# Index heads scored in pairs between the products of a gate projection, and the index's last 72 columns computed feature-major

## What is computed

```python
q, k, v, z, qi, ki, wi = jnp.split(xn @ w_in, cuts, axis=-1)   # 4 x 1024, 8 x 64, 64, 8 columns
qi = concat([rope(qi[..., :32]), qi[..., 32:]])                # 8 index heads of 64
ki = concat([rope(ki[..., :32]), ki[..., 32:]])                # one index key of 64
wi = wi * (8 ** -0.5 * 64 ** -0.5)
rel = relu(einsum("qhd,sd->qhs", qi_b, ki_b))
score = einsum("qh,qhs->qs", w_b, rel)                         # per block of 128 queries
top_val, top_idx = top_k(where(chunk_visible, score, -inf), 128)
...                                                            # softmax attention over the picked keys
return (o * silu(z)) @ w_out
```

## Time and profile before

| | |
|---|---|
| median of 3 runs | 3107.18 us |
| profiled execution, first to last instruction | 3119.8 us |
| PE busy | 3027.5 us (97%) |
| DVE busy | 1790.2 us (57%) |
| POOL busy | 1547.0 us (50%) |
| ACT busy | 928.5 us (30%) |
| mean granted TensorE clock | 0.984 of full |

### The profile page before, as it was taken

One profiled execution on the slowest core, in us unless ns is written; L12 is line 12 of the kernel. 1 busy time (PEld: TensorE's weight loads), 2 busy tenths in 40 slices (PEclk: granted clock), 3 DMA queues, 4 the chain that ended last, 5 costly groups with the idle time before them and its releaser, 6 DMA issues.

```text
span 3119.8 us, 40047 instructions
## 1 busy us (share of the span) xinstructions
PE 3027.5 (97%) x15372; PEld 1965.7 (63%) x15516; DVE 1790.2 (57%) x3290; ACT 928.5 (30%) x1472; POOL 1547.0 (50%) x788
## 2 busy tenths in 40 slices
PE   8999999899999999998999999999999999999998
PEld 6888686688667887886778444455545444444444
DVE  6433398635653433014621999689995456655564
ACT  2001214623661012114222322343333332223222
POOL 5664268955015666466456443345644333443342
PEclk9998799999999999999999999999999999999999
DMA  3222122122332223222122434355555765556551
GB/s 146 108 81 96 44 108 71 26 97 71 132 139 108 108 85 125 95 81 102 55 108 101 183 139 157 149 229 216 202 202 228 243 215 203 191 198 215 208 193 57
DMA packets 139991, 429.99 MB, mean 138 GB/s; under 512 B 8800, under 2 KB 79584, under 8 KB 116704
## 3 DMA queue, kind: packets, MB, share of 16 engines
q1 hardware_dynamic: 125376, 353.40, 31.8%
q10 hardware_dynamic: 7200, 68.68, 5.3%
q0 software_dynamic: 7296, 6.31, 0.9%
HBM read 358.10 MB, written 73.40 MB: 138 GB/s over the span
## 4 chain that ended last, share of the span: by engine, by line
PE 86%; POOL 5%; DVE 4%; issue 3%; DMA 1%; ACT 1%; SPq 0%; DVEq 0%; ACTq 0%; POOLq 0%
PE bank L1140 13%; PE bank L1141 13%; PE bank L1142 13%; PE bank L691 4%; PE bank L692 3%; PE bank L694 3%; POOL rpb_tiles L2459 3%; PE bank L952 3%; PE bank L947 3%; PE bank L948 3%; PE bank L721 3%; PE bank L722 2%; PE bank L749 2%; PE bank L726 2%; PE bank L743 2%
## 5 line engine op out<-in xcount | busy, mean ns | idle before, releaser
L2504 POOL TENSOR_TENSOR work<-ring,work 128x4096 bf16<-128x4096 f32 x64 | 582.8, 9106 | 791.7 <-ACT work L1589 791.7
L1140 PE MATMUL bank<-work 128*128 128x512 bf16 x2005 | 761.1, 380 | 5.7 <-DVE work L2345 2.7
L1141 PE MATMUL bank<-work 128*128 128x512 bf16 x2005 | 761.4, 380 | 3.3 <-ACT work L1600 1.0
L1142 PE MATMUL bank<-work 128*128 128x512 bf16 x1990 | 755.6, 380 | 2.3
L2528 POOL CAST w_parts<-ring 128x1024 fp32r<-128x1024 f32 (+3 forms) x212 | 231.6, 1092 | 652.9 <-DMA ring<-in_wstream 150.6
L2530 POOL TENSOR_TENSOR w_parts<-ring,w_parts 128x1024 fp32r<-128x1024 f32 (+3 forms) x212 | 511.5, 2413 | 17.0
L2345 DVE TENSOR_TENSOR work<-hF,work 128x512 bf16<-128x512 f32 x128 | 307.8, 2405 | 252.5 <-ACT work L1674 249.4
L1142 PEld LDWEIGHTS bank<-work 128*128 128x128 bf16 x2048 | 200.6, 98 | 242.4 <-issue 1.4
L1140 PEld LDWEIGHTS bank<-work 128*128 128x128 bf16 x2048 | 200.7, 98 | 238.7 <-issue 4.7
L1141 PEld LDWEIGHTS bank<-work 128*128 128x128 bf16 x2048 | 200.6, 98 | 234.6 <-issue 1.4
L2313 DVE SCALAR_TENSOR_TENSOR work<-const,work 128x256 f16<-128x256 f32 x512 | 299.1, 655 | 30.0 <-PE bank L1164 29.8
(11 more groups left out here) (424 smaller groups left out, 4942.2 us busy)
## 6 DMA issues: line engine op xcount, KB each, us to landing
ring<-in_wstream SPq DMA_DIRECT2D x128, 2048.0 KB, 7.7
hidden<-hF ACTq DMA_DIRECT2D x32, 1024.0 KB, 3.9
gates<-work ACTq DMA_DIRECT2D x16, 2048.0 KB, 8.8
hF<-hidden SPq DMA_DIRECT2D x32, 1024.0 KB, 7.1
work<-gates SPq DMA_DIRECT2D x32, 1024.0 KB, 10.2
rpb_tiles<-in_rpb POOLq DMA_DIRECT2D x192, 16.0 KB, 2.3
work<-rpb_tiles POOLq DMA_DIRECT2D x24, 128.0 KB, 4.4
ring<-in_wstream SPq DMA_DIRECT2D x5, 512.0 KB, 4.0
```

The lines of the kernel that those rows point to most:

```text
L1140: pe.matmul(out, a(0), b(0), start=(start and k == 0), stop=False)
L1141: pe.matmul(out, a(0), b(1), start=False, stop=False)
L1142: mm = pe.matmul(out, a(1), b(0), start=False, stop=(stop and k == n - 1))
L2504: nc.gpsimd.tensor_tensor(SPLIT[:, p, 1, :], ring[:, p, :], SPLIT[:, p, 0, :], ALU.subtract).then_inc(lo, 1)
```

## The change

1. The last 72 index columns are computed feature-major: 72 weight columns stationary, 512 tokens streaming, into 72 rows of bank 4. There are 24 products in two chunks where there were 96. ACT copies the result to `idx_wide`, PE turns it back by four transposes behind gate chunk 0 (`turn_index_key`), and DVE copies it to `B_IDX`.
2. The index heads are turned two at a time into 128 rows, and the key is doubled (`idx_twice`), so that its transposes fill both halves. That makes 20 transposes in five groups where there were 36 in nine. Four groups stand between gate chunks 3 and 4, the fifth behind chunk 4.
3. The 24 scores become 12 pairs, one head on rows 0 to 63 and one on rows 64 to 127. A pair stands behind every fifth product of gate chunks 5 to 7, the last behind the 60th of their 72. ACT's list has the ReLUs between its Silus. DVE's adds and its selection are as before.

```diff
-        idx_q = area(8192, IDX_HEADS, S)
+        idx_q = area(8192, IDX_HEADS // 2, S)
+        idx_twice = area(10240, NT, 2 * IDX_DIM)
+        idx_wide = area(10752, S)
         idx_k = area(24192, S)
+        IDX_LAST = IDX_COLS - 512
+        IDX_PAIRS = (NT - 1) * IDX_HEADS // 2
+        PAIR_EVERY = 5
...
             def project_index():
                 c = CHUNK["b_idx"]
-                for m, (width, per) in enumerate(((512, 2), (72, 4))):
-                    for k in range(0, KT, per):
-                        token_chunk(c, (FIRST["b_idx"] + m) % 2, range(k, k + per), KT - 1, width, b_rounded, rest,
-                                    signal("b_idx_ready"), "b" if m == 0 else None)
-                        c += 1
-                        if m == 0:
-                            turn_fill("b", k // per)
+                for k in range(0, KT, 2):
+                    token_chunk(c, 0, range(k, k + 2), KT - 1, 512, b_rounded, rest, signal("b_idx_ready"), "b")
+                    c += 1
+                    turn_fill("b", k // 2)
+                out = bank[0:IDX_LAST, 4, :]
+                for ks in (range(4), range(4, KT)):
+                    w = chunk_parts(c, 4, IDX_LAST)
+                    pe.wait_ge(signal("parts_made"), c + 1)
+                    for k in ks:
+                        pe.matmul(out, w[0][:, k % 4, :], b_rounded[:, k, :], start=(k == 0), stop=False)
+                        pe.matmul(out, w[1][:, k % 4, :], b_rounded[:, k, :], start=False, stop=False)
+                    for k in ks:
+                        mm = pe.matmul(out, w[0][:, k % 4, :], rest[:, k, :], start=False, stop=(k == KT - 1))
+                    mm.then_inc(signal("parts_used"), 1)
+                    c += 1
+            def turn_index_key():
+
+                pe.wait_ge(signal("b_idx_by_act"), 3)
+                for t in range(NT):
+                    mm = pe.transpose(bank[:, 5, t * IDX_LAST:(t + 1) * IDX_LAST],
+                                      idx_wide[0:IDX_LAST, t * P:(t + 1) * P], ident[0:IDX_LAST, 0:IDX_LAST])
+                mm.then_inc(signal("b_idx_ready"), 1)
+            def turn_index_pair(i, b):
+
+                for t in range(NT):
+                    x = idx_twice[:, t, :] if i == 0 else B_IDX[:, t, (i - 1) * P:i * P]
+                    mm = pe.transpose(bank[:, b, t * P:(t + 1) * P], x, ident)
+                mm.then_inc(signal("idx_turned"), 1)
+            def score_index_pair(n):
+
+                qt, pair = 1 + n // (IDX_HEADS // 2), n % (IDX_HEADS // 2)
+                size = (qt + 1) * P
+                if n < 2:
+                    pe.wait_ge(signal("idx_turn_taken"), (2, 5)[n])
+                else:
+                    pe.wait_ge(signal("idx_relued"), 2 * n - 2)
+                for e in range(2):
+                    rows_ = slice(64 * e, 64 * e + 64)
+                    pe.matmul(bank[:, 2 * (n % 2) + e, 0:size], idx_q[rows_, pair, qt * P:(qt + 1) * P],
+                              idx_k[rows_, 0:size], start=True, stop=True).then_inc(signal("idx_scored"), 1)
+            def gate_and_index():
+
+                c0, by_act = CHUNK["b_in"], signal("b_in_by_act")
+
+                def gate(j):
+
+                    out, w, done = bank[:, j, :], chunk_parts(c0 + j, KT, P), 24 * (j - 5)
+
+                    def pair_behind(n):
+                        if j >= 5 and (done + n) % PAIR_EVERY == 0 and (done + n) // PAIR_EVERY <= IDX_PAIRS:
+                            score_index_pair((done + n) // PAIR_EVERY - 1)
+
+                    pe.wait_ge(signal("parts_made"), c0 + j + 1)
+                    for k in range(KT):
+                        pe.matmul(out, w[0][:, k, :], b_rounded[:, k, :], start=(k == 0), stop=False)
+                        pair_behind(2 * k + 1)
+                        pe.matmul(out, w[1][:, k, :], b_rounded[:, k, :], start=False, stop=False)
+                        pair_behind(2 * k + 2)
+                    for k in range(KT):
+                        mm = pe.matmul(out, w[0][:, k, :], rest[:, k, :], start=False, stop=(k == KT - 1))
+                        if k == KT - 1:
+                            mm.then_inc(signal("parts_used"), 1)
+                        pair_behind(2 * KT + k + 1)
+
+                for j in range(4):
+                    pe.wait_ge(signal("b_idx_by_act" if j < 2 else "b_idx_by_dve"), j % 2 + 1)
+                    gate(j)
+                    if j == 0:
+                        turn_index_key()
+                pe.wait_ge(signal("idx_rotated"), 1)
+                for i in range(4):
+                    pe.wait_ge(by_act, i + 1)
+                    turn_index_pair(i, i)
+                gate(4)
+                pe.wait_ge(signal("idx_turn_taken"), 3)
+                turn_index_pair(4, 2)
+                for j in range(5, 8):
+                    gate(j)
+                pe.wait_ge(signal("idx_relued"), 2 * IDX_PAIRS)
...
-            def index_scores():
...
-            pe.wait_ge(signal("b_idx_by_act"), 4)
-            pe.wait_ge(signal("b_idx_by_dve"), 4)
-            project_features("b_in", CHUNK["b_in"], FIRST["b_in"], b_rounded, rest)
-            index_scores()
+            gate_and_index()
             for i in range(1, 4):
                 project_b(i)
...
+            def move_index_key():
+
+                act.wait_ge(signal("parts_used"), CHUNK["b_idx"] + 6)
+                act.activation(idx_wide[0:IDX_LAST, :], bank[0:IDX_LAST, 4, :], ACT.Copy)\
+                    .then_inc(signal("b_idx_by_act"), 1)
+            def gate_and_index():
+
+                def gate(j):
+                    take_gate("b_in", "b_in", B_Z, [(j, j)])
+
+                def move(i, b):
+                    act.wait_ge(signal("idx_turned"), i + 1)
+                    act.activation(idx_q[:, i - 1, :] if i else idx_k, bank[:, b, :], ACT.Copy)\
+                        .then_inc(signal("idx_turn_taken"), 1)
+
+                def relus(pairs):
+                    for n in range(2 * pairs[0], 2 * pairs[-1] + 2):
+                        size = (2 + n // IDX_HEADS) * P
+                        act.wait_ge(signal("idx_scored"), n + 1)
+                        if n >= 2:
+                            act.wait_ge(signal("idx_added"), n - 1)
+                        act.activation(idx_rel[:, n % 2, 0:size], bank[:, n % 4, 0:size], ACT.Relu)\
+                            .then_inc(signal("idx_relued"), 1)
+
+                for j in range(4):
+                    gate(j)
+                for i in range(4):
+                    move(i, i)
+                gate(4)
+                move(4, 2)
+                for j in range(3):
+                    end = [min(24 * (x + 1) // PAIR_EVERY, IDX_PAIRS) for x in (j - 1, j)]
+                    relus(range(*end))
+                    gate(5 + j)
...
-            take_tokens("b_idx", lambda m, t: B_IDX[:, t, m * 512:m * 512 + [512, 72][m]], [512, 72])
-            take_gate("b_in", "b_in", B_Z, [(j, j) for j in range(8)])
-            index_scores()
+            take_tokens("b_idx", lambda m, t: B_IDX[:, t, 0:512], [512])
+            move_index_key()
+            gate_and_index()
...
-            take_tokens("b_idx", lambda m, t: B_IDX[:, t, m * 512:m * 512 + [512, 72][m]], [512, 72], [4, 6])
-            dve.wait_ge(signal("b_idx_by_act"), 4)
-            dve.wait_ge(signal("b_idx_by_dve"), 4)
+            take_tokens("b_idx", lambda m, t: B_IDX[:, t, 0:512], [512], [4])
+            dve.wait_ge(signal("b_idx_ready"), 4)
+            order(v.tensor_copy(B_IDX[:, :, 512:IDX_COLS],
+                                bank[:, 5, 0:NT * IDX_LAST].rearrange("p (t n) -> p t n", t=NT)))
+            dve.wait_ge(signal("b_idx_by_act"), 2)
+            dve.wait_ge(signal("b_idx_by_dve"), 2)
             for t in range(NT):
                 rope(B_IDX[:, t, 0:576].rearrange("p (h d) -> p h d", h=9)[:, :, 0:32], 16,
                      plain(trig[:, 2, t, 0:16], trig[:, 3, t, 0:16]), area(B_FREE, 576))
                 order(v.tensor_scalar(B_IDX[:, t, 576:584], B_IDX[:, t, 576:584],
                                       IDX_HEADS ** -0.5 * IDX_DIM ** -0.5, None, ALU.mult))
+            order(v.tensor_copy(idx_twice.rearrange("p t (a d) -> p t a d", a=2),
+                                B_IDX[:, :, 512:576].rearrange("p t (a d) -> p t a d", a=1)
+                                .broadcast_to([P, NT, 2, IDX_DIM])))
             dve.sem_inc(signal("idx_rotated"), 1)
             index_scores()
             selection()
```

More of the change, by code:

```diff
@@ L773, in project_b @@
                         token_chunk(c0 + 8 * (i - 1) + 4 * p + q, p, range(2 * q, 2 * q + 2), KT - 1, 512, b_rounded, rest, ready)
-            def index_scores():
[L777 to L796, removed]
-                pe.wait_ge(relued, n)
             def attention(a, modulated=()):
@@ L1410, in head_roots @@
                 act.activation(sums, sums, ACT.Sqrt, scale=1.0 / dim, bias=eps).then_inc(signal("heads_root"), 1)
-            def index_scores():
```

(17 more changed lines are left out.)

## The result

| | before | after |
|---|---|---|
| timed together, median (lowest to highest) | 3106.93 us (3102.97 to 3113.42), 5 runs | 3087.22 us (3083.80 to 3089.55), 5 runs |
| second time | 3109.14 us (3101.18 to 3124.43), 29 runs | 3088.54 us (3085.96 to 3093.74), 6 runs |
| profiled execution, span | 3119.8 us | 3087.7 us |
| its mean granted clock | 0.984 | 0.991 |

The ratio is 0.9927, interval 0.9902 to 0.9951, and the second time 0.9935, 0.9917 to 0.9952. The change saves 20 us. The forecast was 3072 us with a range of 3063 to 3084: direction right, time 15 us too low, outside the range.

The account below looks back on a forecast made before the run. PE was taken to bound the kernel, with 86% of the chain. Removing 103.8 us and adding 68.7 us gave 35.1 us less, off the 3107.2 us median: 3072 us, range 3063 to 3084.

Parts of the forecast that it names:

- Together 103.8 us: PE time removed: 72-column products 16.9, gate chunks with their wait 47.4, transposes 6.5, scores 30.0, slow start of `project_b` 3.0.
- 3.0 us of slow start: At the start of `project_b`: 16 products take 3.7 us warm but 6.7 us before the change, so 3.0 are lost.
- 24 products of 72 columns and the wait on POOL: Ahead of gate chunk 0: 5.5 us for the feature-major products, then 1.3 us waiting for POOL's parts.
- Five chunks and the transposes: Gate chunks 0 to 4 warm at 5.53 us each, 24 transposes at 3.3 us in all, and 0.3 us of waiting.
- The wait on `idx_rotated`: Before the head transposes: DVE ends near 301.1, PE arrives at 303.9; 0.3 us taken, bounds 0 and 3.
- 12 pairs: In gate chunks 5 to 7: 11.5 us from attention b's rows plus 2.4 us for neighbouring products, taken as 14.0 us.
- rival C: ACT and DVE set the pace of chunks 5 to 7, through adds held by POOL: gain 30, 3077 us, chance 0.09.
- rival B: Thin products or half-array scores bring 1.2 GHz again: one fall 3081 us, chance 0.10; chunks 5 to 7 whole 3103, 0.02.
- POOL late next: At `b_out`: attention b starts 1.4 us less early than POOL's chain, so PE's 3.65 us wait shrinks to about 2.3.
- Rival D: Each of 24 changes between full products and half-array scores stops PE far longer; at 2 us each 3118 us, chance 0.03.
- A: Within a pair the two heads run one after the other: pairs cost 22.6 us, gain 26.5, 3081 us, chance 0.12.
- B's single fall: The clock falls to 1.2 GHz once for some 17 us, costing 8.5: gain 26.6, 3081 us, chance 0.10.

Follow-up runs that it names:

- the profiles with 4 and 8 more products: Kernel before with 4 or 8 extra full products, later overwritten, ahead of the last 72 columns: medians 3109.89 and 3110.58 us, ratios 0.9997 and 1.0002.
- the second profile of after: The changed kernel run once more, unchanged, with a profile: median 3088.54 us in 6 runs, ratio 0.9935.
- its shifted kin: Kernel before with 4, 8 or 12 extra full products ahead of the last 72 columns: medians 3109.89, 3110.58 and 3110.93 us.
- the columns alone: Against before, only the 72 columns made feature-major, transposes and single-head scores kept in one block behind the gate: 3093.23 us, ratio 0.9946.
- the second profile: The kernel before run once more, unchanged, with a profile: median 3105.26 us in 12 runs, ratio 0.9997, profiled span 3123.8 us.
- the three spacings: The changed kernel with a pair behind every fifth product (3088.54 us again), every third (3086.99 us), or two pairs behind every tenth (3084.98 us).

## Why the prediction was wrong

**The step that failed** is "Together 103.8 us", with "I take the difference off it" behind it. The sum counted 30.0 us of scores and 3.0 us of slow start from one execution and subtracted them whole from a median that mostly does without them. The working even had the 12.6 us by which the profile exceeded the median, and called them a difference to be taken off both sides. They were most of the very cost that the sum then removed a second time. Like for like it was more, since a span is about 1.8 us short of a time: 3121.6 against 3107.2, 14.4 us. The term that was mis-sized is 29.32 us for the 24 scores, which take 15.76 at full clock, with the 3.0 us behind them, which are then nothing.

With the scores at full clock, as the profiles with 4 and 8 more products have them, what goes is 103.8 - 13.6 - 3.0 = 87.2 us. What comes is the forecast's 68.7. That makes 18.5 us, and 3107.2 - 18.5 = 3088.7, against 3087.2 and 3088.5 measured. With what the new stretch really takes, 6.74 + 30.26 + 29.33 = 66.3 us, it is 3086.3. Compared with the long runs of before alone, the change is worth nearly what was forecast: 3121.4 - 3088.5 = 32.9 us of 35.1. So is the stage: it takes 113.4 - 0.9 = 112.5 us in the kernel with 4 products more and 112.8 - 1.8 = 111.0 in that with 8, against 90.0 after, 21 to 22.5 us less. The rival that something outside takes the time back falls with it: `project_b` lost 2.9 us where the forecast had 3.0, and attention b grew by 0.5, at a clock of 0.90 instead of 0.95. In the second profile of after attention b took 104.8 us, at a clock of 0.87, yet that span is no longer (3086.8 us).

The 72-column products are the other piece at half clock, and there the profile could be trusted: the clock fell there in every profile of before and its shifted kin. So the 16.9 us and the slow start of gate chunk 0 behind them (7.9 us for it instead of 5.53, 2.4 us) went against 6.74, which makes 12.6 us, and the columns alone brought 12.7.

Point by point:

- *24 products of 72 columns and the wait on POOL*: 277.37 to 284.11, 6.74 us; forecast 6.8, with PE waiting 1.01 us where 1.3 stood.
- *Five chunks and the transposes*: 284.11 to 314.37, 30.26 us; 31.3 in the sum (27.7, 3.3 and 0.3). The transposes took 1.83 us for the 16, and 0.44 and 0.25 for the others, less than taken from attention b.
- *The wait on `idx_rotated`*: none. DVE was done at 306.55, PE came at 306.80. The margin is 0.25 us, where the working (301.1 and 303.9) had 2.8. The stretch itself starts 3.1 us later than in before; beyond that PE came when expected and DVE 2.4 us later.
- *12 pairs*: 29.33 us for chunks 5 to 7, less 3 x 5.53, is 12.7 us; forecast 14.0. The pairs themselves are 10.1 of it, where attention b's distances gave 11.5, and the products beside them lose 0.2 us a pair, as taken.
- *The Trainium skill's rule* ("TensorEngine Tiling (Array Packing)", Key Properties: a change of mode drains TensorE) agrees with the trace in kind: the product ahead of and the product behind a pair take 0.1 us more each, and the pair has 0.2 us that two pairs together pay only once. That is 0.2 us a change and 4.8 for the 24, so the estimate of 4.2 us was near. My 2.4 was not the whole price of the changes; by this reckoning the rest of it was within attention b's 11.5.
- *ACT and DVE hidden* (rival C): yes. The first step of the adds for the second query block takes 2.26 us while POOL's TENSOR_TENSOR runs (the one for the third, with 512 columns, took 0.49), and no wait of PE follows it. DVE and POOL of after in order of time:

```profile
325.21 2.26 DVE L2018 TENSOR_SCALAR work<-work 128x384 f32<-128x384 f32 x1 [1.31 <-ACT work L1488]
```

```profile
324.88 2.37 POOL L2611 TENSOR_TENSOR w_parts<-ring,w_parts 128x1024 fp32r<-128x1024 f32 x1
```

- *The clock* (rival B): none fell in the changed stretch in the profiles of after. But attention b ran at 0.50 for 17.1 us from 481 on and for 3.4 at its end in after's, for 6.8 and 3.4 us in before's.
- *POOL late next*: PE's wait at `b_out` is 0.58 us, not 2.3. In the profiles with a pair behind every third product and two behind every tenth, where attention b's clock is 0.95, it is 3.65 and 3.26, about as in before. So the wait goes with attention b's clock, and the 1.4 us that the forecast took off it do not show. The wait of 2.35 us for DVE stayed.
- *Rival D* is out: a change costs 0.2 us, not 1.6.
- *The chances* did not add up: the forecast, A, B's single fall and C have 0.93 between them, while near 0.15 was said to lie outside the range that holds them.

## What to carry to other kernels

Before a profiled cost is subtracted from a timed median, compare the span of that execution with the median. Here it was 12.6 us above, 14.4 like for like, and every microsecond at a clock of 0.50 in it was a candidate. A stretch at half clock is a cost of that execution; whether it is one of the kernel takes a second profile, or the clocks of the timed runs. Where the half clock is there in each (thin 72-column products), making the work fat pays twice, by less work and by the clock.

## What the runs showed that I had not expected

TensorE can stay at 1.2 GHz while it is never idle. In the earlier trace rows PE was busy 13.41 of 14 us with scores and stayed at 0.50, in the second profile 14.00 of 14, and the same scores ran at 1.00 in three other profiles. So a busy row says nothing about which level is granted.

One and the same kernel has executions of 3099 to 3127 us on two chips, and their mean clocks of 0.983 to 0.991 largely order them. After the change the spread is 10 us in 11 runs, and 15 us (3078.5 to 3093.7) in all 28 of the three spacings. The change made the kernel steadier as well as faster.

Two heads of 512 columns on two halves of the array take 1.06 us, against 1.91 in series: a factor of 1.8, not 2. Two pairs back to back take 1.92 us, so what keeps it from 2 is the 0.2 us that a place costs once.
